# GpSimd takes VectorE's multiply of the gate sums for expert blocks 64 to 127, between its lower activation parts

## The reference, cut to what matters

```python
e = i1 * PEER_NKEYS + i2                    # 16 experts of 8 heads for each token
g = jax.nn.softmax(cv.astype(jnp.float32), axis=-1)
act = jax.nn.gelu(jnp.einsum('td,thkd->thk', xc, u[e]))
return jnp.einsum('thk,thkd->td', g * act, v[e])
```

## Time and profile before

| what | before |
|---|---|
| median of 3 runs | 1052.27 us (1052.14 to 1052.61) |
| profiled execution, span | 1050.2 us |
| TensorE busy | 1045.1 us |
| VectorE busy | 847.5 us |
| ScalarE busy | 731.1 us |
| GpSimd busy | 261.4 us |

### The profile page before, as it was taken

The page is one execution under the profiler, slowest core; times in us unless marked ns, Lnnn a source line. Parts: engine busy times, 40 slices in busy tenths (PEclk is TensorE's granted clock), DMA queues, the critical chain, the costliest instruction groups (busy, mean ns, idle before and its releaser), DMA issues.

```text
span 1050.2 us, 22234 instructions
## 1 busy us (share of the span) xinstructions
PE 1045.1 (100%) x7073; PEld 950.7 (91%) x7073; DVE 847.5 (81%) x1605; ACT 731.1 (70%) x1444; POOL 261.4 (25%) x213
## 2 busy tenths in 40 slices
PE   9999999999999999999999999999999999999998
PEld 7798899989999999999999999988888888888887
DVE  7768886788998889899999999999999995444444
ACT  5556776665544444599889888999999995454453
POOL 0000110017102127600000000134444444545543
PEclk9999999999999999999999999999999999999999
DMA  8643224564555555555444444455544465655553
GB/s 340 254 150 134 91 91 135 190 217 162 161 181 189 186 168 193 179 166 160 160 160 160 160 158 154 140 171 170 169 160 161 167 211 181 200 186 194 199 187 114
DMA packets 50305, 181.34 MB, mean 173 GB/s; under 512 B 5585, under 2 KB 5713, under 8 KB 50257
## 3 DMA queue, kind: packets, MB, share of 16 engines
q1 hardware_dynamic: 50112, 180.59, 51.6%
q10 hardware_dynamic: 144, 0.14, 0.1%
HBM read 178.62 MB, written 2.10 MB: 172 GB/s over the span
## 4 chain that ended last, share of the span: by engine, by line
PE 99%; DMA 0%; ACT 0%; DVE 0%; issue 0%; DVEq 0%
PE bank L862 33%; PE bank L803 12%; PE bank L805 12%; PE bank L804 12%; PE bank L817 5%; PE bank L357 2%; PE bank L358 2%; PE bank L359 2%; PE bank L423 2%; PE bank L743 2%; PE bank L427 1%; PE bank L439 1%; PE bank L440 1%; PE bank L441 1%; PE bank L720 1%; PE bank L721 1%
## 5 line engine op out<-in xcount | busy, mean ns | idle before, releaser
L1644 DVE TENSOR_TENSOR lo<-raw,hi 128x1024 fp32r<-128x1024 f32 x253 | 318.5, 1259 | 123.2 <-ACT hi L1172 122.9
L1172 ACT ACTIVATE hi<-raw 128x1024 fp32r<-128x1024 f32 x253 | 268.1, 1060 | 208.5 <-PE bank L805 113.3
L803 PE MATMUL bank<-xhi,hi 128*128 128x256 f32 x1024 | 292.8, 286 | 0.0
L805 PE MATMUL bank<-xhi,lo 128*128 128x256 f32 x1024 | 290.0, 283 | 0.0
L804 PE MATMUL bank<-xlo,hi 128*128 128x256 f32 x1024 | 289.7, 283 | 0.0
L1904 POOL TENSOR_TENSOR auxl<-big,auxh 128x256 fp32r<-128x256 f32 x126 | 167.7, 1331 | 198.9 <-ACT auxh L1201 198.9
L803 PEld LDWEIGHTS bank<-xhi,hi 128*128 128x128 f32 x1024 | 196.6, 192 | 0.0
L804 PEld LDWEIGHTS bank<-xlo,hi 128*128 128x128 f32 x1024 | 196.3, 192 | 0.0
L805 PEld LDWEIGHTS bank<-xhi,lo 128*128 128x128 f32 x1024 | 196.1, 191 | 0.0
L1188 ACT ACTIVATE oneB<-kep,eT 128x128 fp32r<-128x128 f32 x512 | 162.1, 389 | 0.0
L862 PE MATMUL bank<-hi,auxh 128*128 128x512 f32 x504 | 158.9, 396 | 0.0
(11 more groups left out here) (387 smaller groups left out, 1527.2 us busy)
## 6 DMA issues: line engine op xcount, KB each, us to landing
raw<-u_d SPq DMA_DIRECT2D x128, 512.0 KB, 3.3
raw<-v_d SPq DMA_DIRECT2D x128, 512.0 KB, 3.3
raw<-wpre_d SPq DMA_DIRECT2D x70, 512.0 KB, 4.2
big<-wpre_d SPq DMA_DIRECT2D x8, 512.0 KB, 8.5
big<-x_d SPq DMA_DIRECT2D x4, 256.0 KB, 3.9
out_d<-big SPq DMA_DIRECT2D x2, 512.0 KB, 5.8
big<-out_d SPq DMA_DIRECT2D x2, 512.0 KB, 5.2
out_d<-big SPq DMA_DIRECT2D x4, 256.0 KB, 2.0
```

What stands on the lines that cost most here:

```text
L803: pe.matmul(out, wh, xhi[:, k, :], start=(k == 0), stop=False)
L805: m = pe.matmul(out, wl, xhi[:, k, :], start=False, stop=(k == KT - 1))
L1172: act.activation(hi[:, slot(n), :], raw[:, splits(n) % RING, :], ACT.Copy).then_inc(hi_done, 1)
L1644: dve.tensor_tensor(lo[:, slot(n), :], raw[:, splits(n) % RING, :], hi[:, slot(n), :].bitcast(F32), ALU.subtract).then_inc(lo_done, 1)
```

## The change

In stage 3, `weigh` leaves VectorE's queue (it stays there in stage 2) and becomes `weigh_high` in GpSimd's. GpSimd's order becomes: lower part of tile 0 in halves, of tile 1, multiply of group 64, lower part of tile 2, multiply of group 65, then in each round the lower part of a tile and the multiply of the next group. The wait for "oneA_ready" is dropped. The wait for the last gelu (`bank45_read`) before the first multiply goes from VectorE's queue to GpSimd's. The values that are computed stay the same.

```diff
@@ group_step, VectorE
                 if keys:
                     keys_equal(i, j, base + 3)
-                weigh(i, j, base)
+                if base == 0:
+                    weigh(i, j, base)
                 if rows:
                     rows_a(i, j, base + 2)
@@ between stages 2 and 3, VectorE
             keys_equal(0, 0, NGRP + 3)
-            dve.wait_ge(S("bank45_read"), NH + NBLK // 2)
-            weigh(0, 0, NGRP)
             rows_a(0, 0, NGRP + 2)
@@ GpSimd
-            def w_lo_behind_rows(i, j):
-                pool.wait_ge(S("oneA_ready"), i * UNROLL + (NGRP + SPLIT + j + 1))
+            high_half = big[:, :].rearrange("p (e t) -> p e t", t=T)[:, HALF:2 * HALF, :]
+
+            def weigh_high(i, j):
+
+                g = NGRP + j
+                pool.wait_ge(S("bank67_read"), i * UNROLL + (g + 3))
+                w4 = high_half[:, :, bass.ds(i * (4 * UNROLL) + 4 * j, 4)]
+                pool.tensor_tensor(w4, gsum[:, :, :], w4, ALU.mult).then_inc(S("weighed"), 1)
+
+            def w_lo_and_weigh(i, j):
                 w_lo(i, SPLIT + j)
+                weigh_high(i, j + 2)
 
             w_lo_tokens(0, 0, "whi_tokens", 1, "wlo_tokens")
             w_lo_tokens(0, 1, "whi_done", 1, "wlo_done")
-            for b in range(1, SPLIT):
-                w_lo(0, b)
-            each_tile(pool, HALF - SPLIT, w_lo_behind_rows)
+            w_lo(0, 1)
+            pool.wait_ge(S("bank45_read"), NH + NBLK // 2)
+            weigh_high(0, 0)
+            w_lo(0, 2)
+            weigh_high(0, 1)
+            each_tile(pool, HALF - SPLIT, w_lo_and_weigh)
+            weigh_high(0, NGRP - 1)
             w_lo_tokens(HALF, 0, "whi_tokens", 2, "wlo_tokens")
```

## The result

| what | before | after |
|---|---|---|
| median | 1052.14 us (5 runs, 1051.93 to 1052.61) | 1085.64 us (5 runs, 1085.27 to 1085.9) |
| profiled span | 1050.2 us | 1083.8 us |

The ratio is 1.0317 (95% interval 1.0305 to 1.033): the change costs 33.5 us. The forecast was 1088, of a range from 1053 to 1100.

A forecast was written before the change was run, and what follows sets the result against it. TensorE was taken to bound the kernel at 3.19 us a round; the change makes rounds 3.81, starting v tile 64 36.0 us later: 1052.3 + 36 = 1088 us. Range 1053 to 1100, the forecast's own 1081 to 1095.

The forecast's parts named there:

- What the engines exclude: First half of expert-output stage: GpSimd and VectorE TENSOR_TENSOR exclude each other; VectorE's sum L1778 from PSUM hides GpSimd fully.
- The step from the earlier trace: When GpSimd and VectorE instructions are both queued they take turns; a lead of 0.07 was enough to go first.
- The price of the multiply: GpSimd's 128x256 multiply takes 0.74, as L1904, thus 0.61 after waiting for VectorE; bounds 0.62 and 0.85.
- the rival with 1.15: Rival: runs of four words cost GpSimd more, 1.15 per multiply, 0.41 above the forecast, 62 rounds: 1113 us; chance 0.10.
- The lead of 0.07 to 0.17 over L1769: In each round GpSimd's multiply asks 0.07 to 0.17 before VectorE's row product L1769, so gets the turn.
- The rival that L1769 goes first: Rival: L1769 keeps the turn ahead of the multiply, rounds stay at TensorE's pace: 1052.6 to 1054.6 us; chance 0.22.
- The round: Sum to sum in the stage: 3.81 with lower part L1904 ahead of L1644, 3.24 with it behind.
- The head: Stage start: from the sum at 673.79, 3.62 + 3 x 3.24 + 3.81 puts group 70's sum at 690.9.
- The end: 57 rounds of 3.81, less 2.2, put the last sum at 905.9; v tile 64 starts 36.0 later than 872.79.
- the wait for "oneA_ready" kept the lower part behind L1769: Before the change, this wait made lower part L1904 fall into L1644 and beside the next sum; the change drops it.
- a constant 6 us: Each 0.1 on GpSimd's multiply is worth 6 us; its bounds 0.62 and 0.85 give 1081 and 1095.
- the state that "holds itself up": Rounds of 3.81: as VectorE falls behind, ScalarE's upper part comes earlier in its round, so 3.24 can't last against 3.19.

The follow-up runs named there:

- the two partial kernels: Changed kernel with GpSimd multiplying only half (blocks 64 to 95) or three quarters (64 to 111), the rest left without gates: 1052.41 us and 1074.42 us.
- a wait in the first 24 rounds: Changed kernel with three quarters of the multiply, lower parts waiting for oneA_ready in the first 24 rounds of the loop only: 1052.45 us.
- the kernel where both engines carry the multiply: Changed kernel with VectorE keeping the multiply L1786 and GpSimd running one of 128x256 on unread scratch in the change's place: 1110.63 us.

## Why the prediction was right, and where it was off

*What the engines exclude.* Right. L1769 went from 0.69 to a mean of 1.22 and L1644 from 1.22 to 1.76 (GpSimd group and VectorE groups of 700 to 900 us):
```profile
L1644 DVE TENSOR_TENSOR lo<-raw,hi 128x1024 fp32r<-128x1024 f32 x54 | 94.9, 1758 | 0.0
L1769 DVE TENSOR_TENSOR oneA<-same,gw 128x512 fp32r<-128x512 f32 x54 | 65.7, 1217 | 0.0
...
L1903 POOL TENSOR_TENSOR auxl<-big,auxh 128x256 fp32r<-128x256 f32 x54 | 64.6, 1196 | 0.0
```
The lower part took the forecast 1.2. The step from the earlier trace rows, that queued instructions take turns by when they asked, carried every further run. The Trainium skill (SBUF — State Buffer, Who interferes with whom) names the pair: a VectorE instruction with two SBUF inputs and a GpSimd instruction that reads SBUF, and not a reduction. Both halves agree with the rows here. So the engines do not meet only at semaphores, as the text ahead of the prediction has it: these two also wait for each other inside their instructions.

*The price of the multiply.* Taken as 0.74 from L1904; recorded with 0.74 where VectorE is idle (at 671.79), and with 0.74 to 0.76 in rounds where it asks up to 0.16 before L1760 ends. Runs of four words 1 KB apart cost GpSimd nothing, so the rival with 1.15 falls. The letter of the Trainium skill's rule (GPSIMD Engine Reference, Performance pitfalls for Q7 kernels), which goes by the element step alone, agrees with this trace.

*The lead of 0.07 to 0.17 over L1769.* It was 0.08 (800.90 against 800.98), and enough. This was the narrowest step. The rival that L1769 goes first would have needed GpSimd to be 0.08 later.

*The round.* 3.81 forecast, 3.77 measured (3.765 on average from group 70's sum at 690.87 to group 125's at 897.94). Each stretched instruction ended 0.02 to 0.03 sooner than I took: the stretch is 0.53 to 0.54 for each turn of GpSimd, where my terms came to 0.56. Of the 0.6 that TensorE was to wait in each round, its rows show 0.36 as idle; the rest is overlap of matmuls lost at the restart (L817 to L862 is 0.92 for 0.39, 803.20 to 804.12 against 783.38 to 783.77).

*The head.* Timeline of VectorE's sums and the first stretched L1644 (the answer to the earlier trace rows):
```profile
673.84 0.68 DVE L1778 TENSOR_REDUCE gsum<-bank 128x256 f32<-128x512 f32 x1
...
677.44 0.68 DVE L1778 TENSOR_REDUCE gsum<-bank 128x256 f32<-128x512 f32 x1
...
689.19 1.76 DVE L1644 TENSOR_TENSOR lo<-raw,hi 128x1024 fp32r<-128x1024 f32 x1
690.87 0.68 DVE L1778 TENSOR_REDUCE gsum<-bank 128x256 f32<-128x512 f32 x1
```
As forecast: 3.60 for the first round, then three of 3.22, one of 3.77 with the first stretched L1644, and group 70's sum at 690.87 against 690.9.

*The end.* 57 rounds of 0.045 less are 2.6 us: the last sum started at 903.34, not 905.9, and v tile 64 (the answer to the earlier trace rows) at 906.30, not 908.8.
```profile
906.30 0.70 PE L862 MATMUL bank<-hi,auxh 128*128 128x512 f32 x2 [1.69 <-POOL auxl L1910]
```
That is 33.5 later than 872.79 and the whole of the difference. The forecast was 36.0, and the 2.5 over are the round's 0.045, which is the term that was mis-sized.

*What the prediction did not see.* It says that in the kernel before, the wait for "oneA_ready" kept the lower part behind L1769. It did not: without it that kernel is unchanged (1052.04), as ScalarE's upper part comes later. The wait matters only once VectorE is late, which is what the multiply on GpSimd makes it. It also gave each 0.1 of the multiply a constant 6 us, down to its lower bound of 0.62. In the two partial kernels half of it (0.48 recorded) is worth all 33 us, and three quarters (0.62 recorded) 11, where the slope gives 7 or 8. The slope holds only while the lower part stays ahead of L1644. And it called the state that "holds itself up" without asking how it could be kept out; a wait in the first 24 rounds does.

## What to carry to other kernels

Before giving work of VectorE to GpSimd, look in the trace for instructions of the two that stretch each other, and draw the round as one queue for both: the order in which they ask decides more than the work. In these traces a GpSimd instruction was free beside VectorE's reduction from PSUM (0.68 and 0.74, both as alone), and cost VectorE 0.53 to 0.54 of its 0.74 wherever it got the turn ahead of a VectorE instruction with two SBUF inputs. So a wait that looks idle may be what holds it there. And where the slack of a round is a tenth of a microsecond (3.08 against 3.19 here), a late start can push it into a slow order that it doesn't leave; give the round its order by a semaphore.

## What the runs showed of the hardware

A lead of 0.06 or 0.07 us decided which of the two instructions goes first, both ways (701.12 against 701.18, 704.13 against 704.20).

In the changed kernel TensorE's clock stood at its full level though TensorE was idle for 0.36 in each round of 3.77 for 200 us. In the profiled executions it fell once, in the kernel where both engines carry the multiply, behind the wait of 2.82 us ahead of v tile 64, after some 200 us of rounds in which TensorE was busy five sixths of the time (the stretches of that kernel, columns as in the page, PEclk after POOL):
```profile
800.00:900.00 100.00, 83.66 (x391) 65.54 (x390) 100.00 (x123) 74.93 (x172) 41.19 (x49) 1.00 0.38 126
926.00:930.00 4.00, 1.18 (x6) 0.71 (x5) 3.96 (x5) 1.87 (x4) 2.93 (x3) 1.00 0.49 184
930.00:933.50 3.50, 3.50 (x11) 2.72 (x10) 0.51 (x1) 0.00 (x0) 2.20 (x3) 0.52 0.78 219
933.50:937.00 3.50, 3.50 (x17) 2.90 (x16) 1.23 (x1) 1.46 (x3) 1.27 (x1) 0.99 0.22 85
```
For about 3.4 us it was at 1.2 instead of 2.4 GHz. What that cost, from the timeline of TensorE:
```profile
929.57 0.71 PE L862 MATMUL bank<-hi,auxh 128*128 128x512 f32 x2 [2.82 <-POOL auxl L1911]
930.11 1.02 PE L862 MATMUL bank<-lo,auxh 128*128 128x512 f32 x2
...
933.99 0.62 PE L862 MATMUL bank<-hi,auxh 128*128 128x512 f32 x2
934.45 0.62 PE L862 MATMUL bank<-lo,auxh 128*128 128x512 f32 x2
```
From 930.11 to 933.99 five pairs of matmuls start, in 3.88 us; behind that a pair takes 0.455, so five take 2.28. The difference is 1.6 us, all of what came behind v tile 64. The four executions of that kernel say the same: the three with a mean clock of 0.998 took 1110.49 to 1110.81 us, the one with 1.000 took 1109.17. So the same kernel had the fall in some executions only. In the changed kernel the wait there was 1.69 us and the clock stayed; that the length of the wait is what made the difference is not shown.
